# Gate matmuls of the RG-LRU on the two row halves of TensorE, with sigmoids over 64 partitions

## What is computed

```python
def _rg_lru(x, h0, w_r, b_r, w_i, b_i, lam):
    xb = x.reshape(Bn, L, LRU_BLOCKS, LRU_BW)        # 16 blocks of 64
    r = jax.nn.sigmoid(jnp.einsum('blnc,ncd->blnd', xb, w_r).reshape(Bn, L, D_LRU) + b_r)
    i = jax.nn.sigmoid(jnp.einsum('blnc,ncd->blnd', xb, w_i).reshape(Bn, L, D_LRU) + b_i)
    log_a = -LRU_C * r.astype(f32) * jax.nn.softplus(-lam.astype(f32))
    a = jnp.exp(log_a)
    u = jnp.sqrt(-jnp.expm1(2.0 * log_a)) * (i * x).astype(f32)
    ...  # h_t = a_t * h_(t-1) + u_t
```

## Time and the profile before

| | us |
|---|---|
| median of 3 runs | 1057.01 |
| lowest and highest | 1054.12, 1059.79 |
| span of the profiled execution, first to last instruction | 1051.9 |
| TensorE busy | 956.5 |
| VectorE busy | 673.3 |
| ScalarE busy | 547.8 |
| GpSimd busy | 255.0 |

### The profile page before, as it was taken

The page is one execution under the profiler, slowest core; times in us unless marked ns, Lnnn a source line. Parts: engine busy times, 40 slices in busy tenths (PEclk is TensorE's granted clock), DMA queues, the critical chain, the costliest instruction groups (busy, mean ns, idle before and its releaser), DMA issues.

```text
span 1051.9 us, 16606 instructions
## 1 busy us (share of the span) xinstructions
PE 956.5 (91%) x5923; PEld 846.4 (80%) x5923; DVE 673.3 (64%) x850; ACT 547.8 (52%) x609; POOL 255.0 (24%) x178
## 2 busy tenths in 40 slices
PE   5999899999999998899999999949999999999960
PEld 3999799888979986799999986737788888888740
DVE  5495669658856974611111115389998989999736
ACT  5645534725442473233333324457778787887622
POOL 1013223413411342434434343001111110101021
PEclk9999999999999999899999999969999999999985
DMA  9453121313222120232332368149999999999725
GB/s 290 136 168 81 46 71 42 104 40 90 60 65 70 40 80 1 71 90 80 88 92 80 98 190 309 60 160 327 413 414 413 415 413 415 413 415 413 298 80 215
DMA packets 146596, 193.15 MB, mean 184 GB/s; under 512 B 14471, under 2 KB 91677, under 8 KB 146434
## 3 DMA queue, kind: packets, MB, share of 16 engines
q1 hardware_dynamic: 139000, 165.27, 45.5%
q0 software_dynamic: 4656, 16.21, 4.1%
q10 hardware_dynamic: 2906, 11.23, 2.7%
HBM read 172.91 MB, written 19.77 MB: 183 GB/s over the span
## 4 chain that ended last, share of the span: by engine, by line
PE 69%; DVE 13%; issue 8%; ACT 4%; DMA 2%; SPq 2%; POOL 1%; DVEq 1%; POOLq 0%; ACTq 0%
PE PJ L455 58%; DVE MEM_R L1915 3%; PE NM L1283 2%; PE PJ L1232 1%; DVE MEM L1667 1%; PE MS L1303 1%; PE MS L1471 1%; SPq L594 1%; PE MS L1265 1%; DMA MEM<-in_x_prompt_dram 1%; PE NM L1419 1%; PE MS L1293 1%; DMA MEM<-expert_rows,MEM 1%; POOL MEM L779 1%; DVE MEM_R L1577 1%
## 5 line engine op out<-in xcount | busy, mean ns | idle before, releaser
L455 PE MATMUL PJ<-MEM_R 128*128 128x272 f32 (+2 forms) x5016 | 806.9, 321 | 16.5 <-ACT MEM L862 4.5
L455 PEld LDWEIGHTS PJ<-MEM_R 128*128 128x128 f32 x5016 | 725.4, 191 | 80.1 <-issue 8.9
L669 POOL TENSOR_TENSOR MEM_R<-RAW,MEM_R 128x1024 fp32r<-128x1024 f32 x72 | 176.2, 2455 | 325.1 <-ACT MEM_R L803 325.1
L1915 DVE TENSOR_TENSOR MEM_R<-CHUNK,MEM_R 128x2048 fp32r<-128x2048 f32 x100 | 224.6, 2287 | 15.4 <-ACT MEM_R L1060 14.1
L1060 ACT CAST MEM_R<-CHUNK 128x2048 fp32r<-128x2048 f32 x100 | 189.3, 1911 | 13.4 <-PE PJ L455 6.1
L803 ACT CAST MEM_R<-RAW 128x1024 fp32r<-128x1024 f32 x81 | 84.4, 1051 | 127.2 <-DMA RAW<-in_w_pb_dram 38.4
L1845 DVE TENSOR_TENSOR MERGED<-PJ,MEM 128x544 f32<-128x544 f32 x16 | 11.6, 724 | 145.0 <-PE PJ L455 145.0
L752 POOL COPY MEM<-MEM 128x1 uint32 (+1 forms) x16 | 19.2, 1199 | 235.1 <-PE MS L1471 235.1
L1667 DVE SCALAR_TENSOR_TENSOR MEM<-MEM 128x548 f32<-128x548 f32 x72 | 58.9, 818 | 8.5 <-DVE MEM L1665 0.9
L1069 ACT CAST MEM_R<-MS 128x1024 fp32r<-128x1024 f32 x17 | 17.3, 1015 | 32.9 <-PE MS L1471 32.9
L860 ACT COPY MEM<-PJ 128x272 f32<-128x272 f32 x24 | 9.2, 382 | 42.8 <-PE PJ L455 42.8
(11 more groups left out here) (305 smaller groups left out, 889.9 us busy)
## 6 DMA issues: line engine op xcount, KB each, us to landing
CHUNK<-in_w_gate_dram SPq DMA_DIRECT2D x34, 1024.0 KB, 9.8
CHUNK<-in_w_up_dram SPq DMA_DIRECT2D x34, 1024.0 KB, 11.5
CHUNK<-in_w_down_dram SPq DMA_DIRECT2D x34, 1024.0 KB, 9.9
RAW<-in_w_in_dram SPq DMA_DIRECT2D x56, 512.0 KB, 3.7
expert_rows<-MEM ACTq DMA_DIRECT2D x16, 512.0 KB, 6.0
expert_rows<-MEM SPq DMA_DIRECT2D x8, 512.0 KB, 5.3
RAW<-in_w_pa_dram SPq DMA_DIRECT2D x8, 512.0 KB, 3.7
RAW<-in_w_pb_dram SPq DMA_DIRECT2D x8, 512.0 KB, 3.6
```

The costliest lines, as they stand in the source:

```text
L455: ins = pe.matmul(out, w(a), x(b), start=first and n == 0, stop=last and n == 2)
L669: tt(lo, raw[slot], hi.bitcast(F32), ALU.subtract).then_inc(lo_done, 1)
L1915: tt(moe_hl[c][1], moe_raw[c], moe_hl[c][0].bitcast(F32), ALU.subtract).then_inc(chunk_lo[c], 1)
```

## The change

The stationary tiles of the gates now have 64 rows and 128 columns. For each half of the rows (`side`, the partitions 0 to 63 or 64 to 127, one block of 64 channels each) the 128 columns hold both gates of that block: on side 0 `r` then `i`, on side 1 `i` then `r`. Pair `m` of `PJ` now belongs to side `m` and holds both gates of one block. TensorE runs half 0 of the frames for side 0 and side 1, then half 1 for both. One wait for both pairs stands ahead of all four matmuls, where each gate had its own. ScalarE does four sigmoids over 64 partitions for each c; the pair is handed back after the second sigmoid that reads it. The zeros in `bd` are not needed, so one memset of the start goes.

```diff
-        bd = at("bd", CT, 2, P)
+        bd = at("bd", CT, P)
...
-        NCONST, NLATE = 12, 13
+        NCONST, NLATE = 11, 13
...
-                        side = slice(64 * half, 64 * half + 64)
-                        sp.dma_start(bd[side, :, m, side], blocks[ds(hd, 1), half].rearrange("a p c d -> p (a c) d"))\
+                        side, cols = (slice(64 * s, 64 * s + 64) for s in (half, m ^ half))
+                        sp.dma_start(bd[side, :, cols], blocks[ds(hd, 1), half].rearrange("a p c d -> p (a c) d"))\
                             .then_inc(bd_in, 16)
...
-            const(pool.memset(bd, 0.0))
...
                 def gates(c):
-                    for m, name in enumerate(("br", "bi")):
+                    sides = slice(0, 64), slice(64, P)
+                    for m, side in enumerate(sides):
                         bank(part_b(hd) + 4 + 4 * c + m)
-                        emptied(act.activation(ri[c][:, m, :].rearrange("p (a n) -> p a n", a=2), pj(m)[:, :, 0:LN_ // 2], ACT.Sigmoid,
-                                               bias=v2t[:, ds(hd * CT + (V2C[name] + c), 1)]))
+                        for n, name in enumerate(("br", "bi")):
+                            ins = act.activation(ri[c][side, n, :].rearrange("p (a n) -> p a n", a=2), pj(m)[sides[m ^ n], :, 0:LN_ // 2],
+                                                 ACT.Sigmoid, bias=v2t[side, ds(hd * CT + (V2C[name] + c), 1)])
+                            if n:
+                                emptied(ins)
 
                 def decay(c):
-                    act.wait_ge(pj_free, part_b(hd) + (2 + 4 + 4 * c + 1))
+                    act.wait_ge(pj_free, part_b(hd) + (2 + 4 + 4 * c + 2))
...
                 for c in range(CT):
                     pe.wait_ge(conv_done, hd * 6 + (2 + 5 + c))
-                    for m in range(2):
-                        pe.wait_ge(pj_free, part_b(hd) + (4 + 4 * c + m + 1))
-                        b = pj(m)
-                        for half in range(2):
-                            last = pe.matmul(b[:, half, 0:LN_ // 2], bd[:, c, m, :], xc[:, c, half * (LN_ // 2):(half + 1) * (LN_ // 2)],
-                                             start=True, stop=True)
-                        last.then_inc(pj_full, 1)
+                    pe.wait_ge(pj_free, part_b(hd) + (4 + 4 * c + 2))
+                    for half in range(2):
+                        for m, side in enumerate((slice(0, 64), slice(64, P))):
+                            last = pe.matmul(pj(m)[:, half, 0:LN_ // 2], bd[side, c, :],
+                                             xc[side, c, half * (LN_ // 2):(half + 1) * (LN_ // 2)], start=True, stop=True)
+                            if half:
+                                last.then_inc(pj_full, 1)
```

## The result

The changed kernel is slower: 1069.87 us median (1067.04 to 1071.24, 6 runs) against 1058.19 us (1054.12 to 1059.83, 6 runs), ratio 1.0121 with a 95% interval of 1.0104 to 1.0138, that is 12.8 us (the two medians are 11.7 us apart). Measured a second time, beside experiments 10 and 11, the ratio was 1.0153 (1.0128 to 1.0177). The forecast was 1071.4 us, 14.4 us over before, range 1065 to 1080.

The account below looks back on a forecast made before the run. Bound: bank pair 0's return to TensorE at c=0, the end of ScalarE's sigmoids at c=1. Head 0's 3.09 us plus 11.34 for heads 1 to 3, 14.4, added to the 1057.0 median, gave 1071.4 us, range 1065 to 1080.

Parts of the forecast that it names:

- The sum: All eight gate blocks: 3.09 us in head 0, 3.78 in each of heads 1 to 3, together 14.4 us slower.
- Start at c=0, heads 1 to 3: First gate matmul also waits for pair 1, which still holds the last rows of v: 0.69 us later.
- Start at c=1: First gate matmul also waits for the output gate's sigmoid to empty pair 1: 0.95 us later, all four heads.
- Entering the row mode: At each gate block, TensorE's switch to matmuls with fewer rows costs 0.10 us.
- One more sigmoid for pair 0: Pair 0 needs two sigmoids before it is free, 0.73 us later; ScalarE's last sigmoid ends 1.21 us later.
- The halves side by side: Gate matmuls of the two row halves run in parallel, so pair 0 fills no later: cost 0.
- C: TensorE's granted clock drops at more or fewer places, moving the time over 3 us beside the forecast; chance 0.20.
- B: Forecast costs stay, and the row halves run one after another: 18 to 20 us, 1075 to 1077; chance 0.18.
- D: Sigmoids over half of the partitions cost half, pitch 0.36 us: together 5.6 us, 1062.6; chance 0.05.
- E: TensorE's shorter gate block is what counts: 5.5 us less, 1051.5; chance 0.03.
- signs of being wrong: Sigmoids much under 0.7 us; TensorE's idle before lines 455 and 1265 growing under 8 us; clock adding over three drops.
- Set-up: At the start, one memset and its signal go: cost 0, at most 0.5 us of gain.

Follow-up runs that it names:

- experiments 10 and 11: Changed kernel with side 0's matmuls first, then side 1's, each with its own wait; then plus three unused matmuls behind each gate block: 1.0110 and 1.0107.
- experiments 1 to 4: Kernel before with joint wait, 1.0053; with four sigmoids, 1.0092; with both, 1.0118; changed kernel with two sigmoids over 128 partitions, 1.0053.
- experiment 3: Kernel before with one wait for both bank pairs and four sigmoids over 64 partitions, weights still of 128 rows: 1.0118.
- experiment 5: Changed kernel with side 0's matmuls first, then side 1's, each with its own wait, four sigmoids kept: 1.0117, later 1.0110.
- the filling: Three unused fp32 matmuls behind each gate block: in the kernel with sides in sequence and own waits, 1.0097, later 1.0107; in the changed kernel, 1.0120.
- the quadrants: Kernel before with each gate matmul split into two of 64 rows by 64 columns, own bank pair, separate wait instruction, one sigmoid per gate: 0.9974, 1053.75 us.
- experiment 4: Changed kernel with one sigmoid over 128 partitions for each bank pair, two instead of four for each c (computes another function): 1.0053.
- experiment 2: Kernel before with each gate's sigmoid done as two over 64 partitions, TensorE's matmuls and waits unchanged: 1.0092.

## Why the prediction was right, by its steps

**The sum.** Forecast 14.4 us, measured 12.8 and, the second time, 16.2 (both by the ratio); the medians, 1069.87 and 1072.68 us, both lie in the stated range. By the profile after, its terms come out as follows.
- *Start at c=0, heads 1 to 3*, forecast 0.69: the gates started 0.20 us before the v rows' last copy, now 0.41 behind it, 0.61.
- *Start at c=1*, forecast 0.95: from the end of the projection (202.50 less the 0.20 of before) to 203.17 it is 0.87. Both starts were 0.08 too high, as I had carried over the 0.13 us from ScalarE's end to a matmul; here it is 0.05.
- *Entering the row mode*, forecast 0.10: from the first gate matmul to the first sigmoid it is 188.57 - 187.23 = 1.34 us, where it was 1.23. In head 0 it is 88.29 - 86.98 = 1.31 against 1.32 before, so there nothing is lost.
- *One more sigmoid for pair 0*, forecast 0.73, and 1.21 for the last one's end: 2.90 us for four at both places, pitch 0.73; 2.90 - 1.70 = 1.20.
- *The halves side by side*, taken as 0 for pair 0: right in effect. The passes ran more closely than I had drawn, as four pairs and not as five slots, but pair 0 is full at the same time either way.
- So head 0 at c=0 is 0.72, heads 1 to 3 1.44 each, and c=1 by ScalarE's end 2.17 in each head: 0.72 + 4.32 + 8.68 = 13.7 us.

The mechanism of the forecast, waits for banks and the sigmoids' number, is what experiments 1 to 4 show. That 13.7 is so near the span's 13.4 is in part luck, because the clock moved in both directions. The forecast said that behind c=1 ScalarE's end counts, and that TensorE then waits for line 1707. In the profile after this holds in head 0 alone (1.3 us for line 1710). In heads 1 to 3 TensorE does not wait there at all: its projection behind the gates ran at the lower clock, 7.79 us for 6.28 in head 1, and it came last itself. In head 1 the rows of scores are these (timeline of TensorE, the kernel before first):

```profile
210.96 1.09 PE L1271 MATMUL MS<-MEM 128*128 128x128 f32 x8
```

```profile
214.14 4.95 PE L1268 MATMUL MS<-MEM 128*128 128x512 f32 x20
219.23 1.09 PE L1274 MATMUL MS<-MEM 128*128 128x128 f32 x8
```

From the first gate matmul of c=1 to the last of these rows it is 219.23 - 203.17 = 16.06 us, where it was 210.96 - 196.60 = 14.36: 1.70 more. In heads 2 and 3 it is 1.60 and 1.80 more, and in head 0 1.29. The sum has 2.17 - 0.87 = 1.30 for it. So the clock added 1.2 us at these three places, and 1.5 at c=0 of head 0, and took 1.5 away in head 2 (see C).

**Rivals.** B (one half after another) fell with the 1.20 us for eight passes. D (half the partitions, half the time) fell with 0.71 us for 64 partitions. E (TensorE's shorter block counts) fell with experiment 3: 0.9 us less of passes per block left the next projection where it was, 2.91 us behind the first gate matmul. Tiling speeds up TensorE and not the evacuation of PSUM: that is what the Trainium skill, TensorEngine Tiling (Array Packing), PSUM Bottleneck, warns of. The trace agrees, with the same 2.91 us for 2.12 and for 1.20 us of passes.

C, the clock, is half right: it moves. In the changed kernel's profile it fell behind blocks at which it had never fallen before, and one of these falls lies bare on the chain (head 0, c=0: 13.84 us for 96 passes, 1.5 more than the 12.32 of head 1). At c=1 of head 0 the projection's slowing is covered, since TensorE waits for line 1710 behind it in any case (1.3 us in the table of waits after, 2.26 us at the same place before), at c=1 of the other heads it is covered in the larger part, and the fall behind the numerators of head 2 is gone: 6.10 us there for 7.56.

By its letter one of the forecast's own signs of being wrong came true: the clock was to add no more than three drops, and the profile has 8 before 430 us for 3, five more. The time stayed in the range all the same, because most of them were covered and one of before was gone. The other two signs did not: the sigmoids take 0.71 us, and TensorE's waits before lines 455 and 1265 for what the change touches grew from 5.3 us (0.9 and 4.4) to 16.1 (14.8 and 1.3).

How much of the time is the clock's in the mean of many executions stays open. Experiments 10 and 11, the one pair on one chip, differ by 0.0003, with intervals of some 0.0025 to either side, so an effect of 0.3% is not excluded; and the two readings of the changed kernel, 1.0121 and 1.0153, lie as far apart.

**Set-up.** TensorE's first matmul starts at 5.18 for 5.64 without the memset. The gates of head 0 start at 86.98 for 87.23, but in the profiles of the other versions they start anywhere from 86.72 to 87.91. Whether any of the gain reached the end was not tried apart; nothing in the sum needs it.

**What experiment 5 taught about its own expectation.** The forecast of 8.6 us was a sum of waits as before, and 12.0 us (the mean of its two readings) came. The waits in its trace are as forecast; the 3.4 us beyond them I put down to the clock. Its mean clock is lower than before by 0.005 and 0.004 in its two sets, which would be 3 us by the executions on record, but the filling did not confirm it. That is open.

## What to carry to other kernels

Matmuls that become cheap behind a wait give nothing: look first at what hands their bank back, and count how many instructions of the emptying engine now stand between full and free. A layout that saves TensorE nearly half of the time of its passes but splits each evacuation in two costs ScalarE twice, since here its time goes by the elements in a row and not by partitions (0.71 us over 4 and over 64 partitions, 0.72 over 128). And a clock that moves can hide or add as much as a term of the sum, so compare several executions before a remainder is explained. If two halves of the array are to be used, let each gate keep its own bank and its own wait, and place the tiles so that one instruction over 128 partitions still empties it: the quadrants are the only form here with halves that was not slower, and its gain of 0.3% is too small to build on.

## What the runs showed of the hardware that was not expected

- fp32 matmuls on the two row halves run in pairs of both passes: eight passes of 274 columns in 1.20 us, against 2.01 on 128 rows. On 64x64 tiles, sixteen passes take 2.07 us.
- The pitch of sigmoids from PSUM was not the same over 128 partitions and over 64. Over 128 the second starts before the first's record ends, two in 1.33 us (0.61 from start to start); over 64, four take 2.90 (0.73). From experiment 4's timeline of ScalarE, head 1:

```profile
185.86 1.33 ACT L915 ACTIVATE MEM<-PJ,MEM 128x548 f32<-128x548 f32 x2 [1.39 <-PE PJ L1232]
```

  Why is open. In experiment 2 the sigmoids read and write the two halves in turn; in the changed kernel two in a row write the same half and read different ones, or read the same half and write different ones, and the pitch is 0.73 there too. In the earlier trace rows, from which I had the 0.73, the two activations read different partitions and are over 4. So it may be the number of partitions or the change of them; I had the right row without knowing why. Of the 1.21 us at c=1, some 0.35 (three pitches) come from this alone.
- TensorE's clock fell at 3 to 8 places in the first 430 us, in kernels that differ little, and in two executions of the changed kernel at different places. It fell behind a wait of 1.6 us (head 0, c=0 of the changed kernel) and not behind the one of 2.26 us in the kernel before. More falls in a profile did not always mean more time (1.0121 with 8, 1.0120 with 3).
